# Gate and up tiles of two more feed-forwards as seven block products

## The reference

```python
x = x + 0.5 * swiglu(rmsnorm(x, g_ffn1), w1_gate, w1_up, w1_down)     # feed-forward 1
x = x + concat(sparse_attention, latent_attention) @ w_out
x = x + 0.5 * swiglu(rmsnorm(x, g_ffn2), w2_gate, w2_up, w2_down)     # feed-forward 2
x = rmsnorm(x, g_final)
ml, mc = split(silu(c) @ w_mod + b_mod, 9), split(silu(c_ctx) @ w_mod + b_mod, 9)
# feed-forward 3, on x and cx alike
x  = x  + 0.5 * ml[2] * swiglu_2(rms_norm(x,  g1) * (1 + ml[1]) + ml[0], ffn1_w_in, ffn1_w_out)
cx = cx + 0.5 * mc[2] * swiglu_2(rms_norm(cx, g1) * (1 + mc[1]) + mc[0], ffn1_w_in, ffn1_w_out)
# convolution and attention branches, then feed-forward 4 on x, then rms_norm
def swiglu(x, wg, wu, wd): return (silu(x @ wg) * (x @ wu)) @ wd
```

## Time and profile before

| what | value |
|---|---|
| median of 3 runs | 2512.41 us |
| profiled execution | 2513.3 us, of which the span of its instructions is 2511.5 us |
| TensorE matmuls busy | 2466.2 us, 98% |
| VectorE busy | 1601.0 us, 64% |
| ScalarE busy | 892.9 us, 36% |
| GpSimd busy | 385.6 us, 15% |
| granted TensorE clock, mean | 0.998 |
| moved by DMA | 250.86 MB, mean 100 GB/s |

### The profile page before, as it was taken

One profiled execution on the slowest core, in us unless ns is written; L12 is line 12 of the kernel. 1 busy time (PEld: TensorE's weight loads), 2 busy tenths in 40 slices (PEclk: granted clock), 3 DMA queues, 4 the chain that ended last, 5 costly groups with the idle time before them and its releaser, 6 DMA issues.

```text
span 2511.5 us, 34548 instructions
## 1 busy us (share of the span) xinstructions
PE 2466.2 (98%) x12700; PEld 2093.7 (83%) x12700; DVE 1601.0 (64%) x2548; ACT 892.9 (36%) x1406; POOL 385.6 (15%) x311
## 2 busy tenths in 40 slices
PE   8999999989999999999999999999999999999998
PEld 7888888766688888888999999888888778899997
DVE  7766666789576543488787666544217753768684
ACT  4222133368432222332332234322323652444443
POOL 2101023020121010310110102103001004211112
PEclk9999999999999999999999999999999999999999
DMA  6444435421234323323334312233232013232332
GB/s 197 145 138 151 147 96 142 101 60 42 84 117 151 94 95 97 104 73 118 110 110 129 92 57 68 86 99 93 91 109 72 22 51 101 67 118 86 117 94 75
DMA packets 372756, 250.86 MB, mean 100 GB/s; under 512 B 23248, under 2 KB 368912, under 8 KB 372624
## 3 DMA queue, kind: packets, MB, share of 16 engines
q1 hardware_dynamic: 372624, 249.10, 32.8%
HBM read 237.73 MB, written 2.10 MB: 95 GB/s over the span
## 4 chain that ended last, share of the span: by engine, by line
PE 87%; DVE 9%; ACT 2%; issue 2%; SPq 0%; POOL 0%; DMA 0%; DVEq 0%; ACTq 0%; POOLq 0%
PE PS L1151 17%; PE PS L1158 17%; PE PS L1153 17%; PE PS L1290 5%; PE PS L1292 5%; PE PS L1291 5%; PE PS L1126 3%; PE PS L1127 3%; PE PS L1129 3%; PE PS L1737 2%; DVE WL L2457 1%; PE PS L1081 1%; DVE RB L2337 1%; PE PS L1729 1%; PE PS L1540 1%
## 5 line engine op out<-in xcount | busy, mean ns | idle before, releaser
L1767 ACT ACTIVATE WH<-RAW 128x2048 fp32r<-128x2048 f32 (+2 forms) x155 | 279.4, 1803 | 389.1 <-PE PS L1158 374.8
L2274 DVE TENSOR_TENSOR WL<-RAW,WH 128x2048 fp32r<-128x2048 f32 (+3 forms) x155 | 349.4, 2254 | 87.2 <-ACT WH L1767 86.4
L1151 PE MATMUL PS<-NH,WH 128*128 128x512 f32 x1248 | 379.6, 385 | 4.6 <-DVE WL L2274 2.1
L1153 PE MATMUL PS<-NH,WL 128*128 128x512 f32 x1248 | 377.6, 384 | 0.0
L1158 PE MATMUL PS<-NL,WH 128*128 128x512 f32 x1248 | 372.6, 384 | 0.0
L1151 PEld LDWEIGHTS PS<-NH,WH 128*128 128x128 f32 x1248 | 230.6, 188 | 52.2 <-issue 5.9
L1158 PEld LDWEIGHTS PS<-NL,WH 128*128 128x128 f32 x1248 | 232.1, 188 | 47.3 <-POOL NL L3221 0.7
L1153 PEld LDWEIGHTS PS<-NH,WL 128*128 128x128 f32 x1248 | 232.1, 188 | 46.7
L3179 POOL CAST HH<-VA 128x512 f32 (+3 forms) x88 | 74.3, 844 | 1245.6 <-DVE VA L2514 585.2
L1151 PE MATMUL PS<-HH,WH 128*128 128x512 f32 (+1 forms) x828 | 237.8, 369 | 3.9 <-POOL HL L3181 2.3
L1153 PE MATMUL PS<-HH,WL 128*128 128x512 f32 (+1 forms) x828 | 237.1, 368 | 0.0
(11 more groups left out here) (436 smaller groups left out, 4568.5 us busy)
## 6 DMA issues: line engine op xcount, KB each, us to landing
RAW<-in_ffn_w_in SPq DMA_DIRECT2D x88, 512.0 KB, 4.7
MW<-in_w_mod SPq DMA_DIRECT2D x72, 512.0 KB, 3.4
RAW<-in_w_in SPq DMA_DIRECT2D x70, 512.0 KB, 3.9
RAW<-in_w_gate SPq DMA_DIRECT2D x44, 512.0 KB, 3.7
RAW<-in_w_up SPq DMA_DIRECT2D x44, 512.0 KB, 4.8
RAW<-in_w_down SPq DMA_DIRECT2D x32, 512.0 KB, 3.9
RAW<-in_ffn_w_out SPq DMA_DIRECT2D x40, 256.0 KB, 3.0
RAW<-in_w_out SPq DMA_DIRECT2D x16, 512.0 KB, 3.9
```

Of the source, the lines that this page charges most:

```text
L1151: pe.matmul(outs[half][x], w[half][0], xh(k), start=i == 0, stop=False)
L1153: pe.matmul(outs[half][x], w[half][1], xh(k), start=False, stop=False)
L1767: act.activation(WH[1 - s][:, 0:cols], RAW[1 - s][:, 0:cols], ACT.Copy).then_inc(w_hi, 1)
L2274: dve.tensor_tensor(WL[1 - s][:, 0:cols], RAW[1 - s][:, 0:cols], WH[1 - s][:, 0:cols].bitcast(F32), ALU.subtract).then_inc(w_lo, 1)
```

## The change

In feed-forwards 1 and 2, chunks 1 and 2 (8 and 6 tiles each, 28 in all) go from `tiles` to `seven_products`, with half = 256 tokens, as in feed-forward 4. Chunk 0 stays ordinary (`classic_first`), and carries the sums on the input side, two operations on 128 x 1024 in each of tiles 1 to 7, ahead of VectorE's product. These sums are put into the columns 512 to 768 of NH, NL, HH and HL, which only feed-forward 3 used. Two of the four sums on the weight side go to new tiles S12, two into RAW in place. The code of these chunks is now written out, where it was a loop of two tiles.

The modulation steps are strung anew: none in the gate and up tiles of chunks 1 and 2, 20 in each of feed-forwards 1 and 2 (chunk 0 and all three projections), 32 in feed-forward 3. The context norm goes from chunk 1 into the last projection of feed-forward 2, two blocks in each tile.

```diff
-BOTH = 5 * KD // 2 + 1
+BOTH = 5 * KD // 2
-        M0 = {"ffn1": 0, "ffn2": NF + 8, "ffn3": NF + 20}
+        M0 = {"ffn1": 0, "ffn2": BOTH, "ffn3": 2 * BOTH}
-        MOD_CHUNKS = [bg for bg, _ in ffn3]
+        MOD_CHUNKS = [bg for bg, _ in ffn3] + [ffn1[0][0], ffn2[0][0]]
...
+        SV1 = Seven("ffn1", ffn1, CHUNKS, T, CHUNKS[0], 0)
+        SV2 = Seven("ffn2", ffn2, CHUNKS, T, CHUNKS[0], SV1.u1)
...
+            def classic_first(sv, g0, h0, m0):          # VectorE
+                b0 = sv.stages[0][0]
+                sums = halves_by_steps(sv)
+                for b in range(b0, b0 + sv.plain):
+                    j, s = b - b0, b % 2
+                    if j:
+                        mods(b0, j, s, m0)
+                    if b:
+                        split(s, b)
+                    if j == 0:
+                        mods(b0, j, s, m0)
+                    else:
+                        next(sums)
+                        next(sums)
+                    dve.wait_ge(gate_done, g0 + j + 1)
+                    wait(dve, h_split, after(h0 + j, -1))
                     dve.tensor_tensor(VA[:, s, 0:T], SA[:, s, 0:T], U[s][:, :], ALU.mult).then_inc(psum_free, 1)
                     mods_out(b0, j, s, m0)
...
+            def halves_by_steps(sv):
+                for i in (3, 4, 2):
+                    yield from half_steps(sv, i)        # 3, 3, 2 operations
+                for i in (3, 4):
+                    half_lowered(sv, i)
+                    yield
+                yield from half_steps(sv, 6)            # 2 operations
+                for i in (2, 6):
+                    half_lowered(sv, i)
+                    yield
...
+            def context_scaled(j):
+                for k in (2 * j, 2 * j + 1):
+                    norm_scaled(norm_c1, k)
...
                     if before:
                         before(j)
+                    if before is context_scaled:
+                        norm_low(norm_c1, 2 * j)
+                        norm_low(norm_c1, 2 * j + 1)
...
                     else:                               # ScalarE, in the last projection
                         norm_squares(m, 2 * j - 2, 2 * j)
+                    if m is norm_x1:
+                        norm_high(norm_c1, 2 * j, 2 * j + 2)
...
-                    if m == 7 and sv is SV3:
+                    if m == 7 and sv is not SV4:        # third sum behind the second low part
                         factor_sum(b + 1, 2)
...
-            ffn(ffn1, T, "ffn1", lambda t: 0.5)
+            ffn_sevens(SV1, "ffn1", lambda t: 0.5, None)
-            ffn(ffn2, T, "ffn2", lambda t: 0.5)
+            ffn_sevens(SV2, "ffn2", lambda t: 0.5, None)
```

More of the change, by code:

```diff
@@ L746, in __init__ @@
                 self.u1 = u0
[L748 to L753, removed]
+        SV1 = Seven("ffn1", ffn1, CHUNKS, T, CHUNKS[0], 0)
+        SV2 = Seven("ffn2", ffn2, CHUNKS, T, CHUNKS[0], SV1.u1)
+        SV3 = Seven("ffn3", ffn3, CHUNKS3, T + TC, PLAIN, SV2.u1)
+        SV4 = Seven("ffn4", ffn4, CHUNKS, T, PLAIN, SV3.u1)
+        SEVENS = (SV1, SV2, SV3, SV4)
+        RUNS = {b: r for sv in SEVENS for b, r in sv.runs.items()}
+        for n, sv in enumerate(SEVENS):
+            t = 10 * n
+            sv.t_sum = {3: t + 4, 2: t + 8, 4: t + 12, 6: t + 16} if sv is SV4 else {3: t + 3, 4: t + 6, 2: t + 8, 6: t + 10}
+            t = 4 * n
+            sv.t_lo = {3: t + 1, 2: t + 2, 4: t + 3, 6: t + 4} if sv is SV4 else {3: t + 1, 4: t + 2, 2: t + 3, 6: t + 4}
+        W_PART = sum(kn // 2 - 1 for sv in (SV1, SV2, SV3) for kn in sv.chunks[1:])
         HALF, DSH = T // 2, RQ[:, 0:KD // 2]
         def sv_of(b):
-            return SV3 if b < ffn4[0][0] else SV4
+            return next(sv for sv in SEVENS if b < sv.stages[-1][1])
         def unit(b):
@@ L855, in mods @@
                 t = (s + b0) % 2
-                if not (isinstance(j, int) and j + m0 < 2):
+                if j + m0 >= 2:
                     sp.wait_ge(mod_s, j * 8 + 8 * (m0 - 1))
@@ L1875, in seven_products @@
                     act.wait_ge(st_pe, 6 * u + 4)
-                    if sv is SV4 and u > sv.u0:
+                    if sv is not SV3 and u > sv.u0:
                         act.wait_ge(st_top, u)
@@ L1898, in half_high, with classic_first @@
                     h, f = TH[:, n, :, :], TF[:, n, :, :]
-                elif i in (2, 3):
-                    h, f = T12H[:, 3 - i, :, :], T12F[:, 3 - i, :, :]
-                elif i == 4:
-                    h, f = T3H[:, :, :], T3F[:, :, :]
                 else:
-                    h, f = (z[:, 0:KD // 2, sv.half:sv.tok] for z in (NH, NLF))
+                    h, f, _ = half_tiles(sv, i)
                 act.activation(h, f, ACT.Copy).then_inc(t_hi, 1)
+            def classic_first(sv, ahead):
+                b0 = sv.stages[0][0]
+                for b in range(b0, b0 + sv.plain):
+                    j = b - b0
+                    if j or not (ahead or b == 0):
+                        split(b % 2, loaded(b, 1), b)
+                    act.wait_ge(pe_done, b + 1)
+                    wait(act, psum_free, after(b, -1))
+                    act.activation(SA[:, b % 2, 0:T], G[b % 2][:, :], ACT.Silu).then_inc(gate_done, 1)
+                    if j in (2, 3, 4, 6):
+                        half_high(sv, {2: 3, 3: 4, 4: 2, 6: 6}[j])
             def plain_first(sv):
@@ L2667, in ffn_sevens @@
                     m1 = m0 + kn if bg in MOD_CHUNKS else m0
[L2668 removed]
+                    last = sv is SV2 and c == 2
+                    down(bd, sv.tok, by, by_ctx, True, m1, cols=kn * 2 * P, also=ctx_work if sv is SV2 and c == 0 else None,
+                         before=halves_late if sv is SV3 and c == 0 else context_scaled if last else None)
                     m0 = None if m1 is None else m1 + KD // 2
```

219 lines of the change are left out of this document (94 added, 125 removed).

## The result

The changed kernel takes 2520.43 us (median of 7 runs, 2519.03 to 2522.98), the one before 2512.41 us in the same session. The ratio is 1.0033, its 95% interval 1.0021 to 1.0044: slower, by 8 us, where 2503 was forecast, and outside the range of 2495 to 2510. The profiled execution took 2520.43 us, its span 2518.7 us.

The account below looks back on a forecast made before the run. TensorE's matmuls, filling 98% of the span, were taken as the bound. 22.5 - 5.4 - 1.4 - 5.5 - 0.7 = 9.5 us gained gave 2503 us, range 2495 to 2510.

Parts of the forecast that it names:

- Matmuls: Chunks 1 and 2, feed-forwards 1 and 2: 10.88 to 10.08 us a tile, 22.5 us gained over 28 tiles.
- Chunk 0: Half sums, 2.45 us a tile on VectorE, fill its idle time before the product: cost 0, at most 1 us.
- rival 2: VectorE bounds the 28 new tiles, delaying the seventh product; one more GpSimd meeting a tile gives 2520 us; chance 0.08.
- Seams: Four new seams from projection to block products: seventh product waits for L2502's sum, 1.35 us each, 5.4 in all.
- Last projection of the first: First feed-forward's end: added modulation on VectorE, TensorE waiting 1.0 us for a split; cost 1.4 us, bounds 0 and 3.
- Last projection of the second: Second feed-forward's end: modulation plus context norm on VectorE, slowed by GpSimd; cost 5.5 us, bounds 2.4 and 8.
- Third feed-forward: Two more modulation steps, ahead of its fifth chunk's seam, make that seam wait: 0.7 us, bounds 0 and 1.
- All else: Stages outside the named terms, such as the projections between block products: no term in the sum.
- Rival 3: Dear seams (2.6 us each) and last projections (3 and 8 us): no change, 2512 us; chance 0.20.

Follow-up runs that it names:

- c3: b4 with the split (low part of the next weights) put between the two modulation steps in projection tiles that have two: 2490.88 us (0.9915).
- b4: Changed kernel, Z 32 bytes wider, fourth feed-forward's half sums shifted 32, modulation out of last projections, context norm in their tiles 0-2, modulation transposes before X's update: 2492.58 us.
- b3: Changed kernel with Z 32 bytes wider and the last projections' modulation steps moved into the projections of chunks 0 and 1, context norm staying: 2503.43 us (0.9960).
- b1: Changed kernel with Z 32 bytes wider and GpSimd's sums of squares behind the second feed-forward cut to 8 of 512 columns (output wrong): 2498.15 us (0.9945).
- a4: Changed kernel with Z 32 bytes wider and the context norm put back into chunk 1's projection of the second feed-forward (output wrong): 2502.11 us (0.9961).
- a2: Kernel before with Z 32 bytes wider, shifting all tiles behind it, no instruction changed: 2524.14 us (1.0047).
- b2: Changed kernel with Z 32 bytes wider and 32 bytes put in ahead of the fourth feed-forward's half-sum tiles TH, TL, TF, SM: 2510.09 us (0.9989).
- a3: Kernel before with Z 64 bytes wider, shifting all tiles behind it: 2518.15 us (1.0021).
- c2: Kernel before with 32 bytes put in ahead of HL in the first two feed-forwards, HH staying: 2519.34 us (1.0028).

## Why the prediction was wrong

The span of the profiled execution is 7.2 us longer than before. By the prediction's own terms (us, differences of the stages' widths; a1 is the changed kernel with the tiles in their old places):

| term | predicted | after | a1 |
|---|---|---|---|
| 28 tiles as block products, with their seams | -17.1 | -19.1 | -17.8 |
| last projection of the first feed-forward | +1.4 | +2.6 | +2.1 |
| last projection of the second | +5.5 | +13.0 | +14.0 |
| third feed-forward | +0.7 | +1.4 | +1.6 |
| all else | 0 | +9.3 | 0 |
| sum | -9.5 | +7.2 | -0.1 |

- **Matmuls.** Right. In c3, with one wait of 0.38 us left, the four stages take 80.7 to 81.2 and 60.5 us, as the fourth feed-forward's trace said. The Trainium skill's gap (TensorE: Matmul & The Clock Gate, Back-to-back issue gap) would have given 33 us; no run here reaches its 109 and 216 ns, the fastest matmuls taking 119 and 227.
- **Chunk 0.** Right: in the first feed-forward, from the second tile on, 77.02 us for 77.01.
- **VectorE in the block products (rival 2).** Right to set low: no wait in any tile but a run's first.
- **Seams.** The mechanism, the line and the place were right, the size 0.3 us too big, at one seam 0.7: 1.07, 1.08, 0.63 and 1.08 us for 1.35. b4 beside b3 shows the cause: with the transposes ahead of the addition to X the waits go, with the same modulation steps.
- **Last projection of the first.** The mechanism was right, with the wait of 1.0 us where it was said (1.06 at 363.83). The size was +2.1 to 2.6 for 1.4, in bounds of 0 to 3.
- **Last projection of the second: the step that failed.** The order of the steps was right, and so was their length without GpSimd: for no slowing the prediction's sums give 36.3 us to the second half's addition (39.4 - 5.5 + 2.4), and b1 has 35.7. The mis-sized term is the slowing by GpSimd's sums, of which "1.2 added for GpSimd's sums" is one part: 3.1 us in all (5.5 less the 2.4 without it). The changed kernel has 8.7, and a1 9.7. The price of one meeting was read rightly, 0.97 us from its row and 1.03 in the runs, but it was put in once or so for a tile, as if an operation met one sum. The modulation is many short operations in a row, so each sum that comes in the meantime finds another one to hold up: four in the last tile, three in the third. Behind it stood a second error, of 2.6 us: the chain from X to the next stage was kept at its old length less 0.4 us, 5.4. b1 has just that, at a full clock; with the lower clock in it the chain took 8.0. The second half came at 44.4 us (1065.20 - 1020.82) for 39.4, and with the chain that makes the 13.0 for 5.5. The upper bound of 8 was none: no row of before shows modulation beside four sums, and nothing in it stood for a slower chain.
- **Third feed-forward.** The fifth chunk's seam, the mechanism given, has no wait: seven of the eight waits for L2511 are accounted for by the four new seams and the three old ones of the third, the eighth is the fourth feed-forward's. The time lies in projections that read badly placed tiles (33.6 for 33.4 us); in a1 it is one stretch at a clock of 0.83 behind a wait of 2.3 us, which the kernel before has too but at 1.00 in its profile, as have the changed kernel, a4, b1 and b4 in theirs. The clock falls there in a2 too, which has not one instruction changed, so the +1.6 isn't put down to the change; why it falls in some profiles and not in others is not shown.
- **All else, taken as 0: the other step that failed.** Here lie 9.3 us in the changed kernel and nothing in a1: above all the longer projections. By the medians the 32 bytes cost 8.7 us in all. The first line of the diff, BOTH 21 to 20, was read as a matter of modulation steps; that it moves HH and HL wasn't looked at. No row of before could have priced it, but the allocation could have been compared.

The two misses, 8.5 us of the second feed-forward's end (14.0 - 5.5) and 8.7 us of placement, make up the 17.4 us between 2503 and 2520.4; what the other terms missed cancels within 1 us. Rival 3, dear seams and ends, had the nearer picture; its seams of 2.6 us were 1.5 too dear, its end of 8 us 5 too cheap, and that its sum of no change is what a1 measured is luck. So is rival 2's figure of 2520, which the changed kernel hits: what it rests on, a wait in every block tile, is in no trace. With both misses repaired and the seams mended (c3), the kernel gains 21 us, some 1.4 of them by the fourth feed-forward's half sums (b2), twice what was forecast, since the forecast took the costs at the seams and ends (13 us) as the price of the idea, and they were the price of the order.

## What to carry to other kernels

Before costing a change, compare where its tiles lie with where they lay: a tile that shrinks by 32 bytes in front of a matmul operand can cost more than the change gains, and a pad of the same size tells the two apart in one run. Where work is added to an engine that feeds another, sum up all that it has to do in that stretch, with one delay for every operation of the other engine that falls into the stretch, and not one for the stretch: it is the sum against the stretch that decides, and when it is over, the waits, the slower clock behind them and the late chain come together. Small work that only has to be done at some time goes into stretches where its engine idles, in single steps behind what TensorE wants next.

## What the hardware did that was not expected

- A matmul of 512 columns whose moving operand lies 32 or 96 bytes off a multiple of 128 takes 233 ns, 64 bytes off 229 ns, on it 227 ns (a2, after; a3; a1). With one operand of three off by 32, it is 231 ns on the mean of all three, and the matmuls beside the one that reads it are slowed too (c2). Half sums of 256 columns go the other way, 119 ns off and 120 ns on (b2, a1).
- A sum of GpSimd on 128x512 (1.3 to 1.5 us) holds up one VectorE operation on 128x256, which takes 1.5 us in place of 0.48; the next in the row meets the next sum. Eight in a row take 7.37 us beside four sums, and 3.25 alone.
- The granted clock fell to 0.50 within a wait of TensorE of 4.0 us, which followed one of 3.5 us, where the kernel before keeps 1.00 through the same stage. The short matmuls behind it took 2.07 us for 1.16.
